# Gated merge of attention and mLSTM: the order of three pieces of work at the end of each step of the second mixer

## What is computed

```python
proj = h @ w_in + b_in            # gives m_q, m_k, m_v, m_i, m_f, m_o, m_z, g_attn, g_mlstm, ...
qk = silu(causal_depthwise_conv(concat(m_q, m_k)))
h_tilde = mlstm_chunkwise(mq, mk, m_v, m_i, m_f)      # 8 heads, recurrent over chunks
h_m = head_rms_norm(h_tilde, mlstm_norm_w)
h_m = sigmoid(m_o) * h_m * silu(m_z)
branch_m = h_m @ w_branch_mlstm
merged = sigmoid(g_attn) * branch_a + sigmoid(g_mlstm) * branch_m
out = rms_norm(x + merged @ w_out) * final_norm_w
```

## Time and profile before

| what | value |
|---|---|
| median of 3 runs | 1072.31 us (1072.2 to 1073.39) |
| profiled execution, its time | 1072.99 us |
| its span | 1071.3 us |
| PE busy | 1053.1 us, 98% |
| DVE, ACT, POOL busy | 774.6, 539.8, 687.8 us |
| granted TensorE clock | 0.998 of full speed |

### The profile page before, as it was taken

The page is one execution under the profiler, slowest core; times in us unless marked ns, Lnnn a source line. Parts: engine busy times, 40 slices in busy tenths (PEclk is TensorE's granted clock), DMA queues, the critical chain, the costliest instruction groups (busy, mean ns, idle before and its releaser), DMA issues.

```text
span 1071.3 us, 18681 instructions
## 1 busy us (share of the span) xinstructions
PE 1053.1 (98%) x6343; PEld 853.0 (80%) x6343; DVE 774.6 (72%) x1186; ACT 539.8 (50%) x1286; POOL 687.8 (64%) x469
## 2 busy tenths in 40 slices
PE   7999999999999999999999999999999899999997
PEld 6887887877877888888878888888777788788886
DVE  5964785776866967776776686769588647766897
ACT  7544755746646643554445454545466345113543
POOL 3577555556555569668966797569859984635441
PEclk9999999999999999999999999999999999999999
DMA  6225132132151232224313433232329439676424
GB/s 221 71 93 90 41 119 80 41 119 74 44 158 49 80 118 80 83 56 137 119 51 92 126 92 94 88 117 89 102 94 376 137 118 330 205 275 260 166 99 137
DMA packets 122078, 131.79 MB, mean 123 GB/s; under 512 B 7884, under 2 KB 97288, under 8 KB 120472
## 3 DMA queue, kind: packets, MB, share of 16 engines
q1 hardware_dynamic: 107048, 84.42, 25.7%
q10 hardware_dynamic: 14960, 46.47, 12.7%
HBM read 96.16 MB, written 34.70 MB: 122 GB/s over the span
## 4 chain that ended last, share of the span: by engine, by line
PE 88%; POOL 3%; DVE 2%; DMA 2%; ACT 1%; DVEq 1%; POOLq 1%; issue 0%; ACTq 0%; SPq 0%
PE ps L1104 66%; PE ps L1407 5%; PE ps L1011 4%; PE ps L1221 3%; POOL ring_lo L836 2%; PE ps L1202 2%; PE ps L1276 2%; PE ps L1348 1%; POOL t L831 1%; PE ps L1330 1%; PE ps L1345 1%; DVE u_m L2704 1%; PE ps L1342 1%; PE ps L1296 1%; PE ps L1363 1%; DMA ev<-gm_scratch 1%
## 5 line engine op out<-in xcount | busy, mean ns | idle before, releaser
L836 POOL TENSOR_TENSOR ring_lo<-w,ring_hi 128x512 fp32r<-128x512 f32 x144 | 213.3, 1503 | 86.8 <-ACT ring_hi L1539 86.8
L836 POOL TENSOR_TENSOR ring_lo<-t,ring_hi 128x512 fp32r<-128x512 f32 x108 | 152.2, 1414 | 141.3 <-ACT ring_hi L1539 141.3
L1104 PE MATMUL ps<-s_hi,ring_hi 128*128 128x512 f32 x576 | 228.7, 397 | 1.8 <-issue 1.8
L1104 PE MATMUL ps<-s_lo,ring_hi 128*128 128x512 f32 x576 | 225.1, 391 | 0.0
L1104 PE MATMUL ps<-s_hi,ring_lo 128*128 128x512 f32 x576 | 225.0, 391 | 0.0
L1104 PE MATMUL ps<-h_hi,ring_hi 128*128 128x512 f32 x432 | 170.7, 395 | 2.6 <-POOL ring_lo L836 1.4
L1104 PE MATMUL ps<-h_lo,ring_hi 128*128 128x512 f32 x432 | 169.0, 391 | 0.0
L1104 PE MATMUL ps<-h_hi,ring_lo 128*128 128x512 f32 x432 | 168.6, 390 | 0.0
L1539 ACT ACTIVATE ring_hi<-w 128x512 fp32r<-128x512 f32 x144 | 86.7, 623 | 110.4 <-PE ps L1104 93.7
L1104 PEld LDWEIGHTS ps<-s_hi,ring_hi 128*128 128x128 f32 x576 | 108.2, 188 | 26.0 <-issue 5.1
L1104 PEld LDWEIGHTS ps<-s_hi,ring_lo 128*128 128x128 f32 x576 | 108.2, 188 | 22.4
(11 more groups left out here) (317 smaller groups left out, 2072.0 us busy)
## 6 DMA issues: line engine op xcount, KB each, us to landing
w<-in_w_in SPq DMA_DIRECT2D x128, 256.0 KB, 2.9
xs<-in_x SPq DMA_DIRECT2D x8, 512.0 KB, 8.2
ga_scratch<-ev ACTq DMA_DIRECT2D x4, 1024.0 KB, 4.1
u_scratch<-silu_z ACTq DMA_DIRECT2D x8, 512.0 KB, 3.2
c_rows<-c_scratch ACTq DMA_DIRECT2D x8, 512.0 KB, 6.7
ev<-u_scratch SPq DMA_DIRECT2D x8, 512.0 KB, 4.6
u_sums_scratch<-ev ACTq DMA_DIRECT2D x4, 1024.0 KB, 5.0
gm_scratch<-ev ACTq DMA_DIRECT2D x4, 1024.0 KB, 5.1
```

The costliest lines, as they stand in the source:

```text
L836: return nc.gpsimd.tensor_tensor(flat(lo[:]), flat(raw_or_sum[:]), flat(hi[:]).bitcast(F32), ALU.subtract)
L1104: mm = nc.tensor.matmul(ps[:, bank, columns], w[:, k, :], h[:, k, columns], start=(m == 0), stop=(m == PRODUCT - 1))
```

## The change

Three moves in `mlstm_step(p)` for p = 0, 1, 2. On PE, `turn_h` is issued 4 matmuls ahead of the end of the step instead of 14: after 8 of the 12 matmuls of the last product, where it was after 10 of the 12 of the one before it. DVE's place for `gated_h` stays. On ACT, `store_gm` goes from ahead of the handling of product 1 of the last pair to behind that of product 6, the next. On DVE, `gated_z` goes from the second half of chunks 6 and 7, behind the products retired there, to the first half, ahead of them. No instruction is added or taken away.

```diff
@@ -1352,7 +1352,7 @@
                 more(chunks_end(count))
                 if not last:
-                    more(count * PAIR - 14)
+                    more(count * PAIR - 4)
                     turn_h(p)
                 more(count * PAIR)
@@ -1828,9 +1828,10 @@
                 def after_next(q):
                     if q == 0:
-                        store_gm(p)
                         act.wait_ge(mz_used, 6 * (p + 1))
                     after(q, i0 + 4, raw_part(0, 0))
+                    if q == 1:
+                        store_gm(p)
@@ -2639,6 +2640,8 @@
                     if c:
                         denominators(c - 1)
+                    if c in (6, 7) and not last:
+                        gated_z(p, c - 6)
                     if c == 2 and not last:
                         branch_sums()
@@ -2648,8 +2651,6 @@
                         if c in z_chunks:
                             silu_z_part(z_chunks.index(c))
                             dve.drain()
-                        if c in (6, 7) and not last:
-                            gated_z(p, c - 6)
                 retire(chunks_end(count))
```

## The result

The change makes the kernel slower by a quarter of a per cent. The changed kernel takes 1075.6 us (median of 19, 1074.55 to 1080.07), the kernel before 1072.31 (median of 19, 1071.94 to 1076.08): ratio 1.0027, 95% interval 1.0017 to 1.0037, which is +1.8 to +4.0 us. The forecast was 1074.3, so +2.0; the plain medians differ by 3.3, the ratio gives 2.9. In the experiments I give the difference of such medians beside the ratio. No expectation was set in it, and it rests on few executions each (3 to 10 of an experiment's kernel), so it is to be read beside the traces and not alone. The profiled execution took 1074.55 us with a span of 1072.8.

A forecast was written before the change was run, and what follows sets the result against it. PE, busy 98% of the span, was taken as the bound. Per step 0.715 plus 0 to 0.07 less 0.085, about 0.65, three times gave +2.0: 1072.31 + 2.0 = 1074.3 us, range 1072.1 to 1076.4.

The forecast's parts named there:

- the first term: New PE wait at the next step's second product, for `c22` delayed behind `gated_h` in DVE's queue: 0.715 us a step.
- The wait at product 6: PE at the first matmul of the next step's second product: streams at 617.315 instead of 616.60, for late `c22`.
- the margin of 1.55: Time in us by which `c22` could come later in the kernel before without delaying PE at product 6.
- POOL behind `high_4`: POOL starts its six operations 1.6 us late, after ACT's `high_4`, but regains turns from DVE: adds 0 to 0.07 us.
- the deadline of 633.46: When POOL's six operations must be done so PE does not wait at the second pair's first matmul (position 84).
- the 0.085 at position 84: Existing PE wait at a step's second pair's first matmul, 0.085 us a step, to be absorbed as PE runs later.
- the first two taps would be 1.23 long: Sign in the changed profile: DVE's first two taps run undisturbed while POOL idles, 1.23 us each and not 2.06.
- +0.65 each: Net loss per handover from one step to the next, three times; given as 0.63 to 0.70 us.
- Rival 1: POOL's run of six keeps its length, its 1.6 us late start reaches PE: +4.8, 1077.1 us; chance 0.16.
- the gating by o costs nothing: DVE, chunks 6 and 7: gating half a chunk earlier leaves `c22` 0.8 us of margin; cost 0.
- the store costs nothing: ACT's store one product later: cost 0, up to 1 us a step if weights came over 2 us later.
- Rival 3: Store meets the weights, or `c22` in chunk 7 is late: 0.5 to 1 us a step more, about 1076; chance 0.06.

The follow-up runs named there:

- turn0: Kernel before with only the turning of h moved, to 0 matmuls ahead of the step's end instead of 14: 1079.33 us, ratio 1.0063.
- turn8: Kernel before with only the turning of h moved, to 8 matmuls ahead of the step's end instead of 14: 1074.18 us, ratio 1.0003.
- c22_first: Changed kernel, but DVE finishes `c22` before it turns to `gated_h`: 1076.02 us, ratio 1.0021 against the kernel before.
- turn8_store3: Kernel before with the turning 8 matmuls ahead of the end and the store behind the fourth product (q = 3): 1075.96 us, ratio 1.0021.
- gate_only: Kernel before with only the gating by o moved half a chunk forward: 1072.99 us, ratio 1.0000.
- turn4: Kernel before with only the turning of h moved, to 4 matmuls ahead of the end instead of 14: 1075.66 us, ratio 1.0023.
- store_only: Kernel before with only the store moved, behind product 6's handling: 1074.44 us, ratio 1.0018.

## Why the prediction came out as it did

**Right: the bound and the first term.** All of the loss that the traces show is PE standing still; its busy time grew by 0.4 of 1053. The turning began at 611.19 on the clock of the kernel before (611.20 forecast), `gated_h` at 613.14 (613.15), `c22` ended at 617.13 (617.14). The wait at product 6 cost 0.745, against 0.715: the relation of release and stream, taken from position 84, was 0.03 short here. turn0 and turn8 bear out the margin of 1.55 from both sides, c22_first the mechanism.

**Right in kind, 0.1 short: POOL behind `high_4`.** POOL started at 621.11 on the clock of the kernel before, its run regained the turns that taps had taken in its idle time, and it ended at 633.62; the prediction had 621.0 and 633.45 to 633.53. It took the tap as 2.16 later, though by its own sum `c12` was 2.27 later; ACT's tap indeed began at 618.16 and not 618.06. With 2.27 the run ends at 633.56 to 633.64, and POOL is 0.1 to 0.2 past the deadline of 633.46. So the step by which the 0.085 at position 84 is absorbed fell: that wait is nearly as long as before in two of three steps (0.18 and 0.23). The sign that the first two taps would be 1.23 long didn't quite come either: the first took 1.56 beside the end of POOL's earlier block, the second 1.29. Net +0.78, +0.77 and +0.69 for the three steps, and not +0.65 each.

**The turns.** Rival 1 (POOL's run keeps its length, +4.8) did not happen: 621.97 to 634.48 is 12.51, not 13.45. That an operation of one engine holds off the other for a turn and no more is seen in the changed kernel, in turn8 and, the other way round, in turn8_store3. The Trainium skill, "SBUF — State Buffer", section "SBUF: two separate sides", says that a VectorE instruction with two SBUF inputs and a GpSimd instruction that reads SBUF hold a shared port pair exclusively for a whole instruction. The traces agree, with a turn of 2.24 to 2.28 for POOL against 1.28 alone.

**Right: the gating by o costs nothing.** In chunk 7 it ran 592.09 to 594.27, that is 591.23 to 593.41 on the clock of the kernel before (591.3 and 593.3 forecast), and `c22` followed to 595.54, that is 594.68 (594.7 forecast); no matmul waited, and gate_only is at 1.0000.

**Wrong: the store costs nothing because "POOL's chain has over 2 us before PE needs it".** Moving the store alone makes POOL's first sum of weights start 0.9, 1.3 and 2.7 us later in the three steps, and costs 0 to 0.8 a step (+1.3 at equal clock). So the "up to 1 us a step if the weights came over 2 us later" was about the right size, and the condition was wrong: 1.3 us later was enough to cost. POOL's chain has idle time of 0.69 us between the sums and position 84, at 612.11, and none after; I had counted the distance to PE's use of one block and not followed the queue up to the one place where PE already waited. In the changed kernel the cost doesn't show, because of the other move: POOL idles 2.36 us for `high_4` anyway, and comes into its run of six when ACT lets it, not when the weights do. So the forecast of the sum was right by a cover that it didn't name: the turning costs 2.3, the store 1.3, both together 2.3, so the time being close to the forecast is in this part luck. Rival 3, the store collides, is true of the store alone.

**The sum.** Three handovers cost 2.2 to 2.3 us in the trace: PE's last long stretch of matmuls begins at 990.24, where it began at 988.06 (+2.18), and DVE's last instruction 2.19 later. The span grew by 1.5 alone, because the closing transfer landed sooner in this execution. The ratio's interval (+1.8 to +4.0) holds both 2.0 and 2.3 and doesn't tell them apart; turn4 at equal clock (+2.37) is the nearest measurement. The ratio's own value is 2.9 us; the 0.6 beyond the traced steps is inside that interval and not explained. The 2.9 is above the 2.14 us at which the prediction drew the line to "slower", to which it gave 0.45 against 0.52 for a difference too small to tell.

**What stays open.** How the store's place makes the weights late: at q == 3 POOL's waits for weights are 13.9 us and not 17.0, and they differ from step to step, and the store's part and that of the earlier `c_rows` loads weren't taken apart. What a given lateness costs is known, by the 0.69 us of idle time. No version is clearly faster than the kernel before: turn8 has the shortest steps (111.14), worth 0.2 to 0.3 us in the traces and 0.15 at equal clock, below what the runs can tell.

## What to carry to other kernels

When work is moved later in one engine's order, list what stands behind its consumer in the other engine's queue and compute that instruction's end: here the moved transposes cost PE nothing, and the `c22` behind their consumer cost all. For a transfer, follow the queue of the engine that it feeds up to the first place where the bound engine already waits, and count only idle time on the way as slack. Costs of moves aren't additive: two delays of the same consumer cover each other, and undoing one shows the other, so test each part alone, and again with the other delay taken away.

## What the runs showed of the hardware that wasn't expected

- ACT's first instruction of a step starts 0.60 us after DVE's `gated_h` has ended (616.73 to 617.33 in the changed kernel, 616.32 to 616.92 in c22_first), though it waits for nothing else that the profile shows; the wait stands at the end of the step's code. Behind a wait within a step the same engine began 0.19 after the release (`c12` ended at 618.83, `mk_T` began at 619.02). What the other 0.4 are wasn't tried.
- Lateness of POOL can pass on by most of a turn where it meets DVE: a block that ended 1.04 later in its step held a tap for 1.04 more and made the next two operations end 0.97 later (turn8_store3), though they began at the same point of the step.
- A 1 MB store issued 4.2 us later in its step, among full DMA engines, took 8.4 us and not 5.1 to land (medians). With it, and with the two 512 KB loads that this let go 1.15 us sooner, a 256 KB load beside them landed 0.9, 1.3 and 2.7 us later (store_only).
